# Gate slots of the first activations: 512-column products, four banks, sums on VectorE, and gating on GpSimd

## The chip, the cores and the metric

One core of a Trainium2 chip runs the whole program. The metric is device time in microseconds of one execution; three runs of the kernel before gave a median of 3012.91 us. In the profile, PE is TensorE, PEld its weight loads, DVE is VectorE, ACT is ScalarE, POOL is GpSimd and SP is SyncE.

## The reference, cut to what matters

Two transformer blocks run over 256 tokens of width 2048, all in float32. The second block ends in a mixture of 16384 small experts (PEER). Each token picks 16 experts for each of 8 heads and gates them with a softmax:

```python
act = jax.nn.gelu(jnp.einsum('thkd,td->thk', ub, xb), approximate=False) * gb
vb = jnp.take(v, ib, axis=0)
return jnp.einsum('thk,thkd->td', act.astype(vb.dtype), vb)
```

Here `ub` and `vb` are the rows of `u` and `v` of the chosen experts, `xb` the normed tokens and `gb` the gates.

## The kernel before, in words

The kernel gathers nothing. It computes the activation of every expert for every token (`u` times tokens), multiplies it by a gate that is zero for experts not chosen, and multiplies by all of `v`. The 16384 experts are 128 blocks of 128; a block is one slot. There are two halves of 64 slots each, in the order `peer_u0` (activations of the first half), `peer_v0`, `peer_u1`, `peer_v1`.

**A slot.** SyncE streams a 128x2048 tile of weights into `raw`, with two buffers. Full precision comes from splitting each operand in a high and a low part. ScalarE makes the high part `whi` (L1105), VectorE subtracts to get the low part `wlo` (L1786), and TensorE multiplies whi x high tokens, whi x low tokens and wlo x high tokens, over 16 steps of 128 features. ScalarE may write `whi` of slot n+2 once TensorE has done slot n (`slot_used`), and TensorE starts a slot when its low part is there (`raw_free`).

**Two forms of a slot.** `t_slot` issues three products of 256 columns a step (L523) and puts two slots in one PSUM bank, so that two banks serve in turn. `t2_slot` has the high and the low tokens side by side in `hT2`. It issues one product of 512 columns for whi with both (L536) and one of 256 for wlo (L540), and fills a bank of its own; the two 256-column halves must still be added. `peer_u1` and the query phase `wq` use `t2_slot`, and all of `peer_u0` uses `t_slot`.

**The gates.** In slots 0 to 27 of `peer_u0` (`EARLY` = 28) VectorE selects the experts. In slots 28 to 63, the gate slots, TensorE also makes the gate matrix, beside the activations: 64 groups of four tokens. A group is four products of one-hot rows (L1031) into one of banks 4 to 7. `GATE_COUNT` gives 1 group to slots 28, 29, 35, 42, 49 and 56, 2 to the others and none to slot 63. The products of a group are spread over the steps of the slot by `token_gates`. A group's one-hot rows are written by VectorE in `hot_rows` (L2534 and four of L2539), two groups ahead.

For each group, `weigh` on VectorE (L2547) multiplies the gates of the blocks whose activations are already known into `G`. Then `keep_gates` on ScalarE copies the other gates of this half to `G` (L1612) and those of the second half to a staging buffer (L1614), and sends that to HBM.

**Activations of a pair of slots.** In each even slot VectorE scales the pair before it by the tokens' norm, from PSUM (`scale_acts`, L2447), which also frees the bank. ScalarE computes the gelu of that pair (`gelu_parts`): into `G` for the groups not made yet (L1625), and into `gelu_u` for those already made (L1626). `gate_made` on VectorE then multiplies these with the gates in `G` (L2562), 8 columns for each group made.

**Order of the work.** Each engine works through its program in order. VectorE's iteration for gate slot n is this loop:

```python
for slot in range(EARLY, HALF):
    sum_acts(0, slot - 1)
    if slot in SCALED_AT:
        scale_acts(0, SCALED_AT[slot])
    ...
        split("peer_u0", *divmod(slot + 1, RING))
    ...
    for m in groups_of(slot):
        weigh(m, known_acts(slot))
        ...
            hot_rows(m + 2)
    if slot in SCALED_AT and slot + 2 < HALF:
        gate_made(SCALED_AT[slot], groups_of(slot).stop)
```

`sum_acts` does nothing in `peer_u0` before. ScalarE's iteration is `split` of slot n+1, `keep_gates` of each group of slot n, and in even slots `gelu_parts`. At the start of `peer_v0` ScalarE and VectorE make the first activations' high and low parts (L1651, L2607), and TensorE multiplies them with `v` (L1053), which takes all eight banks. `add_experts`, `gate_pair` and all of the second half stay as they are.

GpSimd has some work in the first block (L1731 to L1742) and four products at the end of the program (L1749).

Of the kernel before, what the change touches and what calls it, by code (L numbers as in the profile page):

```python
# [28 lines left out]
ALU = mybir.AluOpType  # L29
# [52 lines left out]
SUMMED = ("peer_u1",)  # L82
SCALED_AT = {n: n // 2 - 1 for n in range(2, HALF, 2)}
# [78 lines left out]
def fills_per_bank(name, n):  # L162
# [3 lines left out]
    if name in ("in_u", "merge", "nsa_out", "in2_m", "in2_n", "peer_u0", "peer_u1"):  # L166
        return (n, n, 0, 0)
# [16 lines left out]
def build_two_blocks(nc, x, stream, cmpw, params, stage1, mixw_in, fnw1, fnw, gates_dram, out):  # L184
# [6 lines left out]
    with ExitStack() as ctx:  # L191
# [294 lines left out]
        def _(pe):  # L486
# [43 lines left out]
            def t2_slot(name, i, s, ready=None, lo_last=False, middle=None, between=None):  # L530

                t = s % 2
                pe.wait_ge(bank_free[s], i + B0[name][s])
# [502 lines left out]
            for slot in range(EARLY, HALF):  # L1036
                groups = groups_of(slot)
                t_slot("peer_u0", *divmod(slot, RING), (lambda k: token_gates(groups, k)) if groups else None)

            def expert_values(half, i, first, last_group, slots=RING):  # L1040
                name = f"peer_v{half}"
                for s in range(slots):
# [3 lines left out]
                    for b in ((1, 0) if first and s == 0 else (0, 1)):  # L1046
                        if first and s == 0 and b == 0:
                            for e in range(4 if f"peer_u{half}" in SUMMED else 2):
                                pe.wait_ge(bank_free[e], B0[name][e])
# [44 lines left out]
        def _(act):  # L1094
# [478 lines left out]
            def scaled_in(half, p):  # L1573

                i, b = divmod(p, 2)
                if f"peer_u{half}" in SUMMED:
                    act.wait_ge(acts_scaled, HALF // 2 * (half if len(SUMMED) == 2 else 0) + p + 1)
# [140 lines left out]
        def _(pool):  # L1718
# [9 lines left out]
            for c in range(2 * NG):  # L1728
# [14 lines left out]
                pool.wait_ge(pooled, c + 1)  # L1743

# [8 lines left out]
        def _(dve):  # L1753
# [672 lines left out]
            def sum_acts(half, n):  # L2426

                if f"peer_u{half}" in SUMMED:
# [7 lines left out]
                    dve.wait_ge(bank_free[s], B0[f"peer_u{half}"][s] + i + 1)  # L2436

            def scale_acts(half, p):

                i, b = divmod(p, 2)  # L2440
                if f"peer_u{half}" in SUMMED:
# [114 lines left out]
            def gate_made(p, made):  # L2556

                j, b = 2 * p, p % 2
                dve.wait_ge(gelu_done, p + 2)
                dve.wait_ge(g_kept, 4 + made)  # L2560
                gb = G[:, 0:made, j:j + 2, :]
                V.tensor_tensor(gb, gb, gelu_u[:, b, :].rearrange("p (j g t) -> p g j t", j=2, t=4)[:, 0:made],  # L2562
                                ALU.mult).then_inc(gated[b], 1)

            for slot in range(EARLY, HALF):
# [11 lines left out]
                if slot in SCALED_AT and slot + 2 < HALF:  # L2577
                    gate_made(SCALED_AT[slot], groups_of(slot).stop)
# [32 lines left out]
            for half in range(2):  # L2611
# [21 lines left out]
                if half == 0:  # L2633
                    gate_made(HALF // 2 - 2, T // 4)
# [5 lines left out]
                else:  # L2640
                    gate_made(HALF // 2 - 1, T // 4)
# [144 lines left out]
```

## Time and profile before

| | |
|---|---|
| runs, us | 3012.56, 3012.91, 3015.38 |
| the profiled execution, us | 3015.2 |
| its span, us | 3013.3 |
| PE busy | 2959.3 us, 98% |
| PEld busy | 2623.3 us, 87% |
| DVE busy | 1838.7 us, 61% |
| ACT busy | 1262.4 us, 42% |
| POOL busy | 44.9 us, 1% |
| granted TensorE clock, mean | 0.996 of 2.4 GHz |

The time of an execution is a little longer than the span from its first to its last instruction. In a timeline a row has the start in us from the span's start, the duration in us, the engine, the line and operation, output and input, their shapes, and in brackets how long the engine had been idle before and what released it. A count `xN` at the end says that the row merges N instructions. A wait "until issue" had no releaser that the profile shows. Matmuls overlap, so the pitch of whole slots tells more than the duration of one product.

### The profile page before, as it was taken

To read this page: it belongs to the slowest core of one execution; us is meant where nothing else is said; L and a number is where in the kernel's file an instruction comes from. 1 tells how busy PE (TensorE), PEld (TensorE's weight loads), DVE (VectorE), ACT (ScalarE), POOL (GpSimd) and SP (SyncE) were. 2 spreads that over 40 slices of the span, in tenths; PEclk is the share of its full clock that TensorE was granted. 3 is DMA by queue.
4 is the path that set the end of the run, shared out by engine and by line. 5 is a ranking of instruction groups with operands and counts; after the bars stand their busy time and mean duration, and the time that the engine had idled before them with its cause. 6 is when DMAs were issued, how large, how long until landed. Compare 5 with 4: busy or idle time off the path is not lost.

```text
span 3013.3 us, 44793 instructions
## 1 busy us (share of the span) xinstructions
PE 2959.3 (98%) x17931; PEld 2623.3 (87%) x17931; DVE 1838.7 (61%) x2562; ACT 1262.4 (42%) x1518; POOL 44.9 (1%) x63
## 2 busy tenths in 40 slices
PE   7999999999999999999999999999999999999998
PEld 6887899999998888778899999988888888888886
DVE  5555555554555656675899888744445666654444
ACT  4334444443334434444444444444443333344444
POOL 0000013000000000000000000000000000000000
PEclk9999999999999999999999999999999999999999
DMA  5555443334445454335454455555556655555554
GB/s 210 195 202 220 170 158 117 126 141 167 176 171 186 179 195 154 127 139 182 169 181 181 175 172 174 181 195 195 193 190 237 243 187 189 181 195 194 190 190 178
DMA packets 90221, 542.96 MB, mean 180 GB/s; under 512 B 9328, under 2 KB 25840, under 8 KB 26352
## 3 DMA queue, kind: packets, MB, share of 16 engines
q1 hardware_dynamic: 70992, 513.94, 47.4%
q10 hardware_dynamic: 19104, 27.27, 2.6%
q8 instruction: 88, 1.44, 0.2%
q14 instruction: 37, 0.30, 0.0%
HBM read 530.69 MB, written 10.49 MB: 180 GB/s over the span
## 4 chain that ended last, share of the span: by engine, by line
PE 91%; DVE 5%; ACT 2%; issue 1%; DMA 0%; ACTq 0%; SPq 0%; DVEq 0%
PE bank L1053 23%; PE bank L523 22%; PE bank L536 17%; PE bank L540 9%; PE bank L622 8%; PE bank L597 3%; DVE wlo L1786 2%; ACT whi L1105 2%; PE bank L795 2%; PE bank L1031 1%; PE bank L662 1%; PE bank L752 1%; DVE R L2539 0%; PE bank L737 0%; DVE hT L1776 0%
## 5 line engine op out<-in xcount | busy, mean ns | idle before, releaser
L1786 DVE TENSOR_TENSOR wlo<-raw,whi 128x2048 fp32r<-128x2048 f32 (+1 forms) x484 | 1103.7, 2281 | 969.1 <-ACT whi L1105 968.1
L1105 ACT ACTIVATE whi<-raw 128x2048 fp32r<-128x2048 f32 (+1 forms) x484 | 921.2, 1903 | 1320.6 <-PE bank L536 474.3
L523 PE MATMUL bank<-hT,whi 128*128 128x256 f32 x4352 | 823.0, 289 | 0.8 <-DVE wlo L1786 0.8
L536 PE MATMUL bank<-hT,whi 128*128 128x512 f32 x2304 | 804.2, 398 | 3.7 <-DVE wlo L1786 2.9
L523 PEld LDWEIGHTS bank<-hT,whi 128*128 128x128 f32 x4352 | 674.9, 191 | 3.7 <-DVE wlo L1786 1.4
L540 PE MATMUL bank<-hT,wlo 128*128 128x256 f32 x2304 | 622.3, 281 | 1.5 <-DVE wlo L1786 1.2
L523 PE MATMUL bank<-hT,wlo 128*128 128x256 f32 x2176 | 615.3, 283 | 0.0
L536 PEld LDWEIGHTS bank<-hT,whi 128*128 128x128 f32 x2304 | 424.4, 188 | 99.8 <-issue 6.5
L540 PEld LDWEIGHTS bank<-hT,wlo 128*128 128x128 f32 x2304 | 434.0, 189 | 14.4 <-DVE wlo L1786 1.7
L523 PEld LDWEIGHTS bank<-hT,wlo 128*128 128x128 f32 x2176 | 415.4, 191 | 0.0
L1053 PE MATMUL bank<-whi,ghi 128*128 128x512 f32 x1016 | 271.5, 389 | 0.0
L1053 PE MATMUL bank<-wlo,ghi 128*128 128x512 f32 x1016 | 271.5, 389 | 0.0
L1053 PE MATMUL bank<-whi,glo 128*128 128x512 f32 x1016 | 271.5, 389 | 0.0
L622 PE MATMUL bank<-whi,hT 128*128 128x512 f32 x768 | 241.9, 393 | 7.1 <-DVE wlo L1786 3.2
L1053 PEld LDWEIGHTS bank<-whi,glo 128*128 128x128 f32 x1016 | 190.7, 188 | 39.6
L1053 PEld LDWEIGHTS bank<-wlo,ghi 128*128 128x128 f32 x1016 | 190.7, 188 | 39.6
L1053 PEld LDWEIGHTS bank<-whi,ghi 128*128 128x128 f32 x1016 | 190.6, 188 | 39.6
L622 PEld LDWEIGHTS bank<-whi,hT 128*128 128x128 f32 x768 | 145.0, 189 | 40.4 <-issue 9.1
L622 PE MATMUL bank<-wlo,hT 128*128 128x512 f32 x384 | 150.1, 391 | 0.0
L1031 PE MATMUL bank<-R 128*128 128x128 f32 x512 | 99.4, 276 | 1.8 <-DVE R L2539 1.3
L597 PE MATMUL bank<-whi,hT 128*128 128x512 f32 x256 | 85.2, 404 | 0.3 <-ACT R L1422 0.3
L622 PEld LDWEIGHTS bank<-wlo,hT 128*128 128x128 f32 x384 | 72.5, 189 | 14.6
(340 smaller groups left out, 2074.1 us busy)
## 6 DMA issues: line engine op xcount, KB each, us to landing
raw<-stream SPq DMA_DIRECT2D x484, 1024.0 KB, 4.8
R<-cmpw ACTq DMA_DIRECT2D x8, 1024.0 KB, 5.0
gates_dram<-R ACTq DMA_DIRECT2D x64, 128.0 KB, 5.0
R<-gates_dram ACTq DMA_DIRECT2D x16, 512.0 KB, 5.5
xres<-x SPq DMA_DIRECT2D x2, 1024.0 KB, 5.9
R<-mixw ACTq DMA_DIRECT2D x1, 1024.0 KB, 6.8
R<-fnw ACTq DMA_DIRECT2D x1, 1024.0 KB, 6.0
raw<-fnw SPq DMA_DIRECT2D x1, 1024.0 KB, 4.9
```

The costliest lines, as they stand in the source:

```text
L523: last = mm(bank[b][:, t * T:(t + 1) * T], w[t][:, ks], x_[:, k, :], start=(at == 0 and n == 0), stop=(at == KC - 1 and n == 2))
L536: return mm(bank[s][:], whi[t][:, k * P:(k + 1) * P], hT2[:, k, :, :].rearrange("p a t -> p (a t)"), start=(k == 0), stop=(k == KC - 1))
L540: mm(bank[s][:, 0:T], wlo[t][:, k * P:(k + 1) * P], hTh[:, k, :], start=False, stop=False)
L597: last = mm(bank[b][:], x_[:, k, ts_], w[t][:, kk * 512:(kk + 1) * 512], start=(k == 0 and n == 0), stop=(k == KC - 1 and n == 2))
L622: last = mm(bank[2 * h + b][:], x_[:, k, ts_], w[t][:, kk * 512:(kk + 1) * 512], start=(k == 0 and n == 0), stop=(k == KC - 1 and n == 2))
L662: last = mm(bank[6 + v][0:NC4, 0:CH], kb[v][:, l, :], cw[n % 2][:, ll * CH:(ll + 1) * CH], start=(l == 0), stop=(l == CB - 1))
L752: last = mm(o, vN1[:, br, k, kv * DH:(kv + 1) * DH], PT[:, a, j * P:(j + 1) * P], start=False, stop=(j == 2 * nb - 1))
L795: last = mm(bank[s][:, e * T:(e + 1) * T], w[t][:, ks], y[:, k, :], start=(k == 0 and m == 0), stop=(k == 7 and m == 2))
L1031: last = mm(bank[4 + m % 4][:, c * P:(c + 1) * P], second_hot[:, at, :], first_hot[:, at, :], start=True, stop=True)
L1053: last = mm(bank[4 * b + c][:], x_[:, t, ts_], w[t][:, c * 512:(c + 1) * 512], start=(first and s == 0 and n == 0), stop=(last_group and s ...
L1105: A(whi[t][:, 0:w], raw[t][:, 0:w], ACT.Copy).then_inc(hi_ready[t], 1)
L1786: V.tensor_tensor(wlo[t][:, 0:w], raw[t][:, 0:w], whi[t][:, 0:w].bitcast(F32), ALU.subtract).then_inc(raw_free[t], 1)
```

## The change

The gate slots 28 to 63 of `peer_u0` use `t2_slot` instead of `t_slot`. Each fills one of the banks 0 to 3, and VectorE adds the two halves of each (`sum_acts`, a reduction from PSUM to `act_in`); the pair is then scaled in place from SBUF. Slots 0 to 27 keep the old form. The products with the gates (`gate_made`) leave VectorE and are issued on GpSimd, with the same operands, for pairs 13 to 31. The counts of bank fills follow.

```diff
+def summed(half, slot):
+
+    return half == 1 or slot >= EARLY
...
+    if name == "peer_u0":
+        return (n, n, n - EARLY // RING, n - EARLY // RING)
...
-            def t2_slot(name, i, s, ready=None, lo_last=False, middle=None, between=None):
+            def t2_slot(name, i, s, ready=None, lo_last=False, middle=None, between=None, skipped=0):
 
                 t = s % 2
-                pe.wait_ge(bank_free[s], i + B0[name][s])
+                pe.wait_ge(bank_free[s], i + (B0[name][s] - skipped))
...
             for slot in range(EARLY, HALF):
                 groups = groups_of(slot)
-                t_slot("peer_u0", *divmod(slot, RING), (lambda k: token_gates(groups, k)) if groups else None)
+                t2_slot("peer_u0", *divmod(slot, RING), between=(lambda k: token_gates(groups, k)) if groups else None,
+                        skipped=0 if slot % RING < 2 else EARLY // RING)
...
-                            for e in range(4 if f"peer_u{half}" in SUMMED else 2):
+                            for e in range(4):
                                 pe.wait_ge(bank_free[e], B0[name][e])
...
-                if f"peer_u{half}" in SUMMED:
-                    act.wait_ge(acts_scaled, HALF // 2 * (half if len(SUMMED) == 2 else 0) + p + 1)
+                if summed(half, 2 * p):
+                    act.wait_ge(acts_scaled, (HALF // 2 if half else 0) - EARLY // 2 + p + 1)
...
+            for p in range(FIRST_GATED, HALF // 2):
+                j, b, made = 2 * p, p % 2, groups_of(2 * p + 2).stop if 2 * p + 2 < HALF else T // 4
+                pool.wait_ge(gelu_done, p + 2)
+                pool.wait_ge(g_kept, 4 + made)
+                gb = G[:, 0:made, j:j + 2, :]
+                nc.gpsimd.tensor_tensor(gb, gb, gelu_u[:, b, :].rearrange("p (j g t) -> p g j t", j=2, t=4)[:, 0:made],
+                                        ALU.mult).then_inc(gated[b], 1)
...
             def sum_acts(half, n):
 
-                if f"peer_u{half}" in SUMMED:
+                if summed(half, n):
...
-                    dve.wait_ge(bank_free[s], B0[f"peer_u{half}"][s] + i + 1)
+                    dve.wait_ge(bank_free[s], B0[f"peer_u{half}"][s] + i + 1 - (0 if half or s < 2 else EARLY // RING))
...
             def scale_acts(half, p):
...
-                if f"peer_u{half}" in SUMMED:
+                if summed(half, 2 * p):
...
-            def gate_made(p, made):
-
-                j, b = 2 * p, p % 2
-                dve.wait_ge(gelu_done, p + 2)
-                dve.wait_ge(g_kept, 4 + made)
-                gb = G[:, 0:made, j:j + 2, :]
-                V.tensor_tensor(gb, gb, gelu_u[:, b, :].rearrange("p (j g t) -> p g j t", j=2, t=4)[:, 0:made],
-                                ALU.mult).then_inc(gated[b], 1)
...
-                if slot in SCALED_AT and slot + 2 < HALF:
-                    gate_made(SCALED_AT[slot], groups_of(slot).stop)
...
-                if half == 0:
-                    gate_made(HALF // 2 - 2, T // 4)
                 sum_acts(half, HALF - 1)
                 scale_acts(half, HALF // 2 - 1)
                 split(name, 0, 1)
                 if half:
                     gate_pair(HALF // 2 - 1)
-                else:
-                    gate_made(HALF // 2 - 1, T // 4)
```

In `peer_u1`, `sum_acts` and `scale_acts` are those of the second half before, L2433 and L2443 in the profile.

## Rows read from the trace of the kernel before

**Rows 1.** Waits, 1675 to 1942 us: total us, times, longest us.

```profile
DVE wlo L1786 <- ACT whi L1105: 37.4, 35, 1.6
...
DVE R L2547 <- PE bank L1031: 5.1, 7, 1.9
PEld bank L1031 <- issue: 3.9, 12, 0.5
```

**Rows 2.** Timeline of ScalarE before slot 28: start us, us, what.

```profile
1657.74 1.92 ACT L1105 ACTIVATE whi<-raw 128x2048 fp32r<-128x2048 f32 x1 [1.90 <-PE bank L523]
1663.51 1.92 ACT L1105 ACTIVATE whi<-raw 128x2048 fp32r<-128x2048 f32 x1 [3.84 <-PE bank L523]
```

**Rows 3.** Timeline of ScalarE in the query phase, first two slots, 512-column products.

```profile
1422.20 1.92 ACT L1105 ACTIVATE whi<-raw 128x2048 fp32r<-128x2048 f32 x1 [0.61 <-PE bank L536]
1427.75 1.92 ACT L1105 ACTIVATE whi<-raw 128x2048 fp32r<-128x2048 f32 x1 [3.63 <-PE bank L536]
```

**Rows 4.** Timeline of ScalarE in the second half's activations, 512-column products.

```profile
2309.48 1.92 ACT L1105 ACTIVATE whi<-raw 128x2048 fp32r<-128x2048 f32 x1 [3.21 <-PE bank L536]
...
2315.12 1.92 ACT L1105 ACTIVATE whi<-raw 128x2048 fp32r<-128x2048 f32 x1 [3.73 <-PE bank L536]
```

**Rows 5.** Timeline of VectorE: its iterations 32, 33 and 62 begin.

```profile
1706.08 0.69 DVE L2447 TENSOR_TENSOR R<-bank,token_scale 128x512 f32<-128x512 f32 x1
1707.53 2.29 DVE L1786 TENSOR_TENSOR wlo<-raw,whi 128x2048 fp32r<-128x2048 f32 x1 [0.77 <-ACT whi L1105]
...
1713.64 0.23 DVE L2562 TENSOR_TENSOR R<-R 128x64 f32<-128x64 f32 x1 [0.18 <-ACT R L1626]
1715.44 2.29 DVE L1786 TENSOR_TENSOR wlo<-raw,whi 128x2048 fp32r<-128x2048 f32 x1 [1.58 <-ACT whi L1105]
...
1931.38 0.68 DVE L2447 TENSOR_TENSOR R<-bank,token_scale 128x512 f32<-128x512 f32 x1
1932.73 2.29 DVE L1786 TENSOR_TENSOR wlo<-raw,whi 128x2048 fp32r<-128x2048 f32 x1 [0.67 <-ACT whi L1105]
```

**Rows 6.** Timeline of ScalarE at the end of gate slot 32.

```profile
1713.37 0.24 ACT L1626 ACTIVATE R<-R 128x64 f32<-128x64 f32 x1
1713.51 1.90 ACT L1105 ACTIVATE whi<-raw 128x2048 fp32r<-128x2048 f32 x1
```

**Rows 7.** Timeline of VectorE: weighings that waited for TensorE, three of seven.

```profile
1688.85 0.27 DVE L2547 TENSOR_TENSOR R<-bank,R 128x112 f32<-128x112 f32 x1 [0.41 <-PE bank L1031]
...
1733.36 0.30 DVE L2547 TENSOR_TENSOR R<-bank,R 128x136 f32<-128x136 f32 x1 [0.39 <-PE bank L1031]
...
1890.39 0.38 DVE L2547 TENSOR_TENSOR R<-bank,R 128x216 f32<-128x216 f32 x1 [0.31 <-PE bank L1031]
```

**Rows 8.** Timeline of TensorE's weight loads: three of its twelve gaps.

```profile
1719.68 0.30 PEld L1031 LDWEIGHTS bank<-R 128*128 128x128 f32 x2 [0.23 <-issue]
...
1869.24 0.30 PEld L1031 LDWEIGHTS bank<-R 128*128 128x128 f32 x2 [0.42 <-issue]
...
1929.63 0.30 PEld L1031 LDWEIGHTS bank<-R 128*128 128x128 f32 x2 [0.51 <-issue]
```

**Rows 9.** Timeline of VectorE in the second half: a sum and a scaling.

```profile
2303.77 0.69 DVE L2433 TENSOR_REDUCE R<-bank 128x256 f32<-128x512 f32 x1 [2.16 <-PE bank L536]
2304.50 0.69 DVE L2443 TENSOR_TENSOR R<-R,token_scale 128x512 f32<-128x512 f32 x1
```

**Rows 10.** GpSimd's groups by line and shape: x count, busy us, mean ns.

```profile
L1749 POOL TENSOR_TENSOR R<-xres,raw 128x512 f32<-128x512 f32 x4 | 5.0, 1288 | 2516.5 <-DVE xres L2654 2516.5
```

**Rows 11.** Timelines of GpSimd and of VectorE, an overlap in the first block.

```profile
455.88 2.34 POOL L1731 COPY R<-R 128x256 f32<-128x256 f32 x1
...
455.12 2.85 DVE L1786 TENSOR_TENSOR wlo<-raw,whi 128x2048 fp32r<-128x2048 f32 x1 [3.00 <-ACT whi L1105]
```

**Rows 12.** Timelines of VectorE and of TensorE at the start of peer_v0.

```profile
1940.68 0.75 DVE L2607 TENSOR_TENSOR glo<-R,ghi 128x256 fp32r<-128x256 f32 x2
...
1942.24 1.09 PE L1053 MATMUL bank<-whi,ghi 128*128 128x512 f32 x4
```

More of the change, by code:

```diff
@@ L165, in fills_per_bank @@
         return (n,) * 4
-    if name in ("in_u", "merge", "nsa_out", "in2_m", "in2_n", "peer_u0", "peer_u1"):
+    if name == "peer_u0":
+        return (n, n, n - EARLY // RING, n - EARLY // RING)
+    if name in ("in_u", "merge", "nsa_out", "in2_m", "in2_n"):
         return (n, n, 0, 0)
```

## The prediction

> **What bounds the kernel.** I read the page's busy shares first: TensorE is busy for 98% of the span at a granted clock of 2.4 GHz in every slice, so only TensorE's own time, or a wait of TensorE, can move the end. Then I read the stretch that the change touches, the 36 gate slots (28 to 63), from about 1675 to 1942 us. The waits there [rows 1] hold the argument. TensorE's weight loads had twelve gaps, 3.9 us together, so the stretch isn't bound by TensorE alone. ScalarE and VectorE hand work round in a ring, and this ring sets the pace of most slots: VectorE's low part of a slot waits for ScalarE's high part 35 times, 37.4 us; VectorE in turn waited for TensorE only 7 times, 5.1 us.
>
> The ring, for slot n: VectorE weighs the slot's last group (L2547); ScalarE keeps the rest of that group, in even slots computes the pair's gelu, and then makes the high part of slot n+2's weights (L1105); VectorE makes their low part (L1786), weighs slot n+1's first group and makes the one-hot rows for slot n+2's first group (L2534, L2539); TensorE's first gate product of slot n+2 needs these rows. Every gap of TensorE is at that product, in an even slot: [rows 8] show those of slots 34, 54 and 62, growing from 0.23 to 0.51 us.
>
> The reader should see two things in VectorE's timeline [rows 5]. In each iteration of its loop VectorE stands idle before L1786, 0.77 and 0.67 us in even iterations and 1.58 us in odd ones, always released by ScalarE. And the gating product that the change takes away (L2562) lies in the odd hole, behind ScalarE's gelu and before that wait.
>
> **TensorE's part.** A slot goes from 48 products of 256 columns to 16 of 512 and 16 of 256. The same columns pass, so the price is read from the pitch of whole slots. A slot of the old form is 1663.51 − 1657.74 = 5.77 us [rows 2], one of the new form 2315.12 − 2309.48 = 5.64 us in the second half [rows 4] and 5.55 us in the query phase [rows 3]. The second half streams the same kind of weights through the same loop of waits, so I take its row, rounded down with the 5.76 of most old slots to 0.11 us a slot, 0.007 us for each of 16 steps; the query phase's 0.21 is the other bound. The 256 gate products are untouched. If TensorE alone set the pace, this would be 36 × 0.11 = 4.0 us (7.6 by the other bound).
>
> It doesn't. What TensorE saves before one of the twelve gaps makes that gap longer: the one-hot rows come when the ring brings them. A saving counts only where the ring itself waited for TensorE. That is so in seven places, of which [rows 7] show three:
> - Slots 28 and 29, before the first gap: 2 × 0.11 = 0.22 us, under the wait of 0.41 in slot 29.
> - The four slots with one group in the middle (35, 42, 49, 56), where VectorE waited 0.39, 0.46, 0.30 and 0.31 us; [rows 7] have the first and the last of these four. From the last gap before each, TensorE has run 30 or 46 steps (slot 34 to 35, [rows 8], is 14 + 16; slot 54 to 56 is 14 + 32), so it arrives 0.21, 0.32, 0.21 and 0.32 us earlier. None may exceed its wait: 0.21 + 0.32 + 0.21 + 0.31 = 1.05 us.
> - After the last gap, in slot 62, TensorE runs freely to the end of slot 63: 30 steps, 0.21 us.
>
> Together −1.5 us. By 0.21 us a slot it would be 0.41 + (0.39 + 0.46 + 0.30 + 0.31) + 0.39 = 2.3 us.
>
> **VectorE's additions.** Each slot gets a sum of the two halves, 0.69 us, and the next operation starts 0.73 us after it because its completion is awaited (2304.50 − 2303.77, [rows 9]). The scaling stays at 0.69 us, now from SBUF: the same [rows 9]. That is 36 × 0.73 = 26 us of added work, and it costs what doesn't fit in the holes. Even iterations: sum and scaling need 0.73 + 0.69 = 1.42 us from where the scaling began; L1786 started 1707.53 − 1706.08 = 1.45 us after that point at the start and 1932.73 − 1931.38 = 1.35 us at the end [rows 5]. So it fits early and is up to 0.07 us too long late; neighbours on VectorE overlap a little, so I take 0.2 us over all 17, between 0 and 17 × 0.07 = 1.2. Odd iterations: the sum waits for the gelu of the pair before (it overwrites that input), which ends at 1713.37 + 0.24 = 1713.61 [rows 6]; 0.73 us later is 1714.34, and L1786 starts at 1715.44 [rows 5] because ScalarE's high part ends then. 1.1 us remain: cost 0. The cover is ScalarE's 1.90 us high part; if it were gone, each odd iteration would pay the 0.73.
>
> Taking the 19 gating products from VectorE (0.23 us for 64 columns, [rows 5]) gives nothing: VectorE went from each into a wait for ScalarE (1.58 us), and ScalarE waited for none of them.
>
> **Banks.** Slots now use four banks in turn; a bank is needed again four slots later and is freed one slot later. 0. At the start of peer_v0 TensorE begins with banks 4 to 7 and needs banks 0 to 3 only after twelve products; four of them take 1.09 us [rows 12], so about 3 us later. The last sum and nothing else is late by 0.73 us: 0.
>
> **GpSimd's products.** GpSimd stood idle here. No row shows a product of this shape (runs of 4 and 8 elements); the nearest is a plain one of 512 columns at 1.29 us [rows 10], 2.5 ns a column. The products have 8 columns for each group made, 8 to 480 in the loop and 512 twice. Each starts when its gelu ends (1713.61) and, if it keeps VectorE out, must be over when L1786 starts (1715.44): 1.83 us, of which I allow 0.1 to start. At 1.29 or less, that is 0. Does it keep VectorE out? [Rows 11] show that the two engines exclude each other for some pairs of operations: a GpSimd copy of 256 columns took 2.34 us and ended with VectorE's low part (455.12 + 2.85 = 457.97), which itself was stretched from 2.29 to 2.85 us. The Trainium skill says so in "SBUF — State Buffer", Who interferes with whom: a VectorE operation with two SBUF inputs and a GpSimd one that reads SBUF exclude each other for a whole instruction, while a reduction on this chip never contends. By that rule the new sum passes beside GpSimd, and the total below stands as it is; the trace agrees for L1786, and has no row for a sum. If the sum were held up too, it would end at 1713.7 + 1.3 + 0.7 = 1715.7 us, 0.3 late, where the product has all 1.29 us, so in the last two or three odd iterations: 0.6 us. I take 0 of it, since a sum reads PSUM alone, and keep 0.6 for the range.
>
> One place is tight. The product of pair 30 starts while VectorE is about to make peer_v0's first low activations (L2607, two in 0.75 us from 1940.68, [rows 12]). TensorE wants the first at 1942.24, now 0.2 us earlier, about 0.9 us after it was ready. A GpSimd product of 1.29 us that slips in ahead would cost 0.4 us, one that doesn't 0. I take 0.1. Later, the waits for gated pairs lie more than a slot after GpSimd's last product: 0.
>
> **Sum.** −1.5 + 0.2 + 0.1 = −1.2 us. The profiled execution has a span of 3013.3 us and a time of 3015.2, which is 2.3 above the median of the runs, 3012.91. The difference is carried to the median: **3011.7 us**, with 3010.6 (−2.3) to 3013.6 (−1.5 + 1.2 + 0.4 + 0.6) for this case from the ends of its terms.
>
> **Rivals.**
> - *The ring gives way.* If VectorE's side without gating made the one-hot rows early enough, the gaps would go and TensorE's saving would be whole: −4.0 − 3.9 = −7.9, 3005.0 us. It would need 0.2 to 0.5 us less in each round. Against it: nothing on ScalarE's side gets shorter, and VectorE waits for ScalarE in 35 of 36 iterations [rows 1].
> - *The sum lies on the ring in even iterations.* If the hole of 0.67 to 0.77 us were not to be had (the sum starting late, or the scaling waiting), 17 × 0.73 = 12.4 us: 3012.9 − 1.2 + 12.4 = 3024 us. It decides once a round grows by 0.42 us. For it: the hole is full to 0.1 us. Against it: the sum's products end well before VectorE comes to it, so it has nothing to wait for.
> - *GpSimd's products outlast the hole.* At twice the plain row (5 ns a column) the five products from 360 to 480 columns average 2.1 us, 0.4 over the 1.7 free, and pair 30's costs 1.7 at the entry: +3.7, 3015.4 us. At three times, nine products exceed it by 1.0 each and the entry pays 3.0: +12, 3024 us. It decides at about 2.4 times. For it: [rows 11], and that no such shape was ever timed. Against: runs of 4 contiguous elements.
>
> **How the numbers follow.** Forecast 0.73; the ring gives way 0.07; the sum on the ring 0.07; GpSimd at up to 2.4 times 0.08, beyond it 0.05. A measurement of this kernel tells a difference from none at about 0.2%, 6 us. Faster than 3006.9: 0.07. Slower than 3018.9: 0.12. Within: 0.81. The range runs from 3007.5, towards the ring's giving way, to 3016.5, past GpSimd's twofold price, and leaves out under 2 in 10.
>
> **What would show it.** L536 and L540 in place of L523 in this stretch, and old-form slots' 5.76 against 5.65 us where no gap is. TensorE's weight loads with twelve or more gaps, each in an even slot, each longer by about 0.1 to 0.2 us, so some 6 us in total instead of 3.9. VectorE's idle before L1786 near 0 in even iterations and about 0.9 in odd ones, still released by ScalarE. GpSimd's products at 1.3 us or less for 480 columns, and L1786 at 2.29 us. I am wrong if L1786 is stretched or released by GpSimd, if the rounds of two slots (7.91 us from 1707.53 to 1715.44 for the first half of one, [rows 5]) change by more than 0.1 us, or if the gaps vanish.

## The result and the profile after

Before: median 3014.39 us of 20 runs (3011.43 to 3016.94). After: 3018.89 us of 20 runs (3015.17 to 3023.32). The ratio is 1.0016, with a 95% interval of 1.0009 to 1.0023: the change makes the kernel slower, by 2.7 to 6.9 us. The forecast was a gain of 1.2 us, and the range ended at 3016.5. The three runs that the forecast started from had a median 1.5 us below that of the twenty, so the difference is the number to explain.

The profiled execution took 3017.41 us with a span of 3015.6 us, against 3015.2 and 3013.3 before, at the same mean granted clock of 0.996. The two traces are laid side by side at six marks: VectorE's first scaling of the gate slots, its last weighing in slot 62, TensorE's first product of `peer_v0`, of `peer_u1` and of `peer_v1`, and VectorE's last operation of the program.

| stretch | before, us | after, us | difference |
|---|---|---|---|
| gate slots (first scaling to last weighing) | 259.26 | 259.46 | +0.20 |
| entry to `peer_v0` (last weighing to first product) | 5.55 | 7.75 | +2.20 |
| `peer_v0` | 349.14 | 349.22 | +0.08 |
| `peer_u1` | 362.28 | 362.29 | +0.01 |
| `peer_v1` | 351.48 | 351.45 | −0.03 |

The loss in these two traces is in two places, 2.4 us together: most of it at the entry, and a small one where a gain was forecast. The waits of after, from 1675 to 1942 us, answer to [rows 1]. Columns: engine, what waits, what ended the wait; total us, times, longest.

```profile
DVE wlo L1804 <- ACT whi L1115: 18.9, 17, 1.1
...
PEld bank L1040 <- issue: 7.1, 12, 0.8
DVE R L2451 <- ACT R L1636: 7.0, 18, 3.4
DVE R L2565 <- PE bank L1040: 4.2, 7, 1.8
```

TensorE's gaps are still twelve but hold 7.1 us instead of 3.9. VectorE waits for ScalarE before its low part 17 times instead of 35, so the even iterations have no idle left there, and only the odd ones (1.1 us each) do. VectorE's wait for TensorE fell only from 5.1 to 4.2. And there is a new line: the sum (L2451) waits for ScalarE's gelu (L1636), once for as long as 3.4 us. The page's row for TensorE's first product of an expert block (`expert_values`, L1063), with its one idle time at the end:

```profile
L1063 PE MATMUL bank<-whi,ghi 128*128 128x512 f32 x1016 | 271.6, 389 | 2.1 <-DVE glo L2614 2.1
```

**The entry.** VectorE's timeline in after, from the end of iteration 62, against the same in [rows 12]. Columns: start us, us, engine and line, shapes, and in brackets the idle time before and what ended it.

```profile
1936.73 0.41 DVE L2565 TENSOR_TENSOR R<-bank,R 128x240 f32<-128x240 f32 x1 [1.26 <-PE bank L1040]
1940.58 0.69 DVE L2451 TENSOR_REDUCE R<-bank 128x256 f32<-128x512 f32 x1 [3.44 <-ACT R L1636]
1941.30 2.69 DVE L1804 TENSOR_TENSOR wlo<-raw,whi 128x2048 fp32r<-128x2048 f32 x1
1943.92 0.75 DVE L2614 TENSOR_TENSOR glo<-R,ghi 128x256 fp32r<-128x256 f32 x2
```

ScalarE, GpSimd and TensorE at the same place, one view each:

```profile
1936.57 1.92 ACT L1115 ACTIVATE whi<-raw 128x2048 fp32r<-128x2048 f32 x1 [0.60 <-PE bank L545]
...
1939.86 0.62 ACT L1636 ACTIVATE R<-R 128x512 f32<-128x512 f32 x1
```

```profile
1940.55 1.29 POOL L1760 TENSOR_TENSOR R<-R 128x512 f32<-128x512 f32 x1 [15.73 <-ACT R L1636]
1946.74 2.61 POOL L1760 TENSOR_TENSOR R<-R 128x512 f32<-128x512 f32 x1 [4.90 <-ACT R L1636]
```

```profile
1944.48 1.17 PE L1063 MATMUL bank<-whi,ghi 128*128 128x512 f32 x4 [2.13 <-DVE glo L2614]
```

Before, the same place has these rows of VectorE and of ScalarE:

```profile
1938.47 2.29 DVE L1786 TENSOR_TENSOR wlo<-raw,whi 128x2048 fp32r<-128x2048 f32 x1 [1.38 <-ACT whi L1105]
```

```profile
1939.82 0.62 ACT L1626 ACTIVATE R<-R 128x512 f32<-128x512 f32 x1
```

In after, ScalarE had the high part of `peer_v0`'s first weights ready at 1938.5. Before, VectorE made the low part there, at 1938.47. Now iteration 63 begins with the sum of slot 62. It writes over the input of pair 30's gelu, and that gelu is not made in iteration 62, as those of other pairs are in their even iteration: `slot + 2 < HALF` fails for slot 62, and ScalarE makes it at the entry, after `keep_gates` and the high activations. So the sum starts at 1940.58. The low part starts 2.83 us later than before and takes 2.69 instead of 2.29 us beside GpSimd's product. The low activations start at 1943.92 instead of 1940.68, and TensorE stands still for 2.13 us.

**The gate slots.** VectorE in iterations 32, 33 and 62 of after answers to [rows 5]:

```profile
1705.90 0.69 DVE L2451 TENSOR_REDUCE R<-bank 128x256 f32<-128x512 f32 x1
1706.62 0.69 DVE L2461 TENSOR_TENSOR R<-R,token_scale 128x512 f32<-128x512 f32 x1
1707.36 2.29 DVE L1804 TENSOR_TENSOR wlo<-raw,whi 128x2048 fp32r<-128x2048 f32 x1
...
1713.54 0.69 DVE L2451 TENSOR_REDUCE R<-bank 128x256 f32<-128x512 f32 x1 [0.24 <-ACT R L1636]
1715.34 2.29 DVE L1804 TENSOR_TENSOR wlo<-raw,whi 128x2048 fp32r<-128x2048 f32 x1 [1.11 <-ACT whi L1115]
...
1931.51 0.69 DVE L2451 TENSOR_REDUCE R<-bank 128x256 f32<-128x512 f32 x1
1932.23 0.69 DVE L2461 TENSOR_TENSOR R<-R,token_scale 128x512 f32<-128x512 f32 x1
1932.86 2.29 DVE L1804 TENSOR_TENSOR wlo<-raw,whi 128x2048 fp32r<-128x2048 f32 x1
```

The even iterations are as forecast: sum and scaling fill the hole, and the low part starts 1932.86 − 1931.51 = 1.35 us after the start of this work, the same as 1.35 in [rows 5]. In the odd ones VectorE has 1.11 us left and is released by ScalarE, also as forecast. Yet look at when it is released. ScalarE's timeline of after has the high part of this slot at

```profile
1713.34 1.90 ACT L1115 ACTIVATE whi<-raw 128x2048 fp32r<-128x2048 f32 x1
```

so the low part starts 2.00 us after the high part did. Before it was 1715.44 − 1713.51 = 1.93 us [rows 5, 6]. It is 2.00 or 2.01 in all 17 odd iterations of after, and 1.93 in all 17 of before. TensorE's weight loads, the gaps of slots 34, 54 and 62, answer to [rows 8]:

```profile
1719.58 0.30 PEld L1040 LDWEIGHTS bank<-R 128*128 128x128 f32 x2 [0.58 <-issue]
...
1869.37 0.30 PEld L1040 LDWEIGHTS bank<-R 128*128 128x128 f32 x2 [0.77 <-issue]
...
1929.76 0.30 PEld L1040 LDWEIGHTS bank<-R 128*128 128x128 f32 x2 [0.82 <-issue]
```

### The profile page after: what moved, and what is told of

Read it like the earlier page. It is cut to its first block, busy times and chain, and to the rows that moved or that the text cites. A ratio compares the mean times of both kernels' runs of the same rounds, so it can differ in the third digit from the quotient of the medians.

```text
span 3015.6 us, 43714 instructions
## 1 busy us (share of the span) xinstructions
PE 2956.9 (98%) x17355; PEld 2593.9 (86%) x17355; DVE 1855.4 (62%) x2579; ACT 1262.4 (42%) x1518; POOL 61.0 (2%) x82
## 4 chain that ended last, share of the span: by engine, by line
PE 89%; DVE 6%; ACT 3%; issue 1%; DMA 0%; ACTq 0%; DVEq 0%; SPq 0%
PE bank L1063 23%; PE bank L545 19%; PE bank L532 18%; PE bank L549 10%; PE bank L631 8%; PE bank L606 3%; DVE wlo L1804 2%; ACT whi L1115 2%; PE bank L804 2%; PE bank L671 1%; DVE R L2557 1%; PE bank L1040 1%; PE bank L761 1%; DVE R L2552 0%; PE bank L746 0%
## 5 line engine op out<-in xcount | busy, mean ns | idle before, releaser
L545 PE MATMUL bank<-hT,whi 128*128 128x512 f32 x2880 | 1021.0, 398 | 3.9 <-DVE wlo L1804 3.0
L545 PEld LDWEIGHTS bank<-hT,whi 128*128 128x128 f32 x2880 | 533.7, 188 | 113.7 <-issue 7.4
L532 PE MATMUL bank<-hT,whi 128*128 128x256 f32 x3200 | 585.5, 285 | 0.8 <-DVE wlo L1804 0.8
L532 PEld LDWEIGHTS bank<-hT,whi 128*128 128x128 f32 x3200 | 498.2, 192 | 3.6 <-DVE wlo L1804 1.4
L1063 PE MATMUL bank<-whi,ghi 128*128 128x512 f32 x1016 | 271.6, 389 | 2.1 <-DVE glo L2614 2.1
L1063 PE MATMUL bank<-wlo,ghi 128*128 128x512 f32 x1016 | 271.5, 389 | 0.0
L1063 PE MATMUL bank<-whi,glo 128*128 128x512 f32 x1016 | 271.5, 389 | 0.0
L631 PE MATMUL bank<-whi,hT 128*128 128x512 f32 x768 | 242.1, 393 | 7.3 <-DVE wlo L1804 3.2
L1063 PEld LDWEIGHTS bank<-whi,ghi 128*128 128x128 f32 x1016 | 190.6, 188 | 41.9 <-issue 2.4
L1063 PEld LDWEIGHTS bank<-wlo,ghi 128*128 128x128 f32 x1016 | 190.7, 188 | 39.7
L1063 PEld LDWEIGHTS bank<-whi,glo 128*128 128x128 f32 x1016 | 190.7, 188 | 39.6
L2451 DVE TENSOR_REDUCE R<-bank 128x256 f32<-128x512 f32 x100 | 69.0, 690 | 69.4 <-PE bank L545 62.3
L1040 PEld LDWEIGHTS bank<-R 128*128 128x128 f32 x512 | 95.3, 189 | 17.1 <-issue 7.1
```

The lines of the kernel that those rows point to most:

```text
L532: last = mm(bank[b][:, t * T:(t + 1) * T], w[t][:, ks], x_[:, k, :], start=(at == 0 and n == 0), stop=(at == KC - 1 and n == 2))
L545: return mm(bank[s][:], whi[t][:, k * P:(k + 1) * P], hT2[:, k, :, :].rearrange("p a t -> p (a t)"), start=(k == 0), stop=(k == KC - 1))
L631: last = mm(bank[2 * h + b][:], x_[:, k, ts_], w[t][:, kk * 512:(kk + 1) * 512], start=(k == 0 and n == 0), stop=(k == KC - 1 and n == 2))
L1040: last = mm(bank[4 + m % 4][:, c * P:(c + 1) * P], second_hot[:, at, :], first_hot[:, at, :], start=True, stop=True)
L1063: last = mm(bank[4 * b + c][:], x_[:, t, ts_], w[t][:, c * 512:(c + 1) * 512], start=(first and s == 0 and n == 0), stop=(last_group and s ...
L2451: last = V.tensor_reduce(act_in[half][:, n % 2 * T:n % 2 * T + T], bank[s][:].rearrange("p (a t) -> p t a", a=2), AX.X, ALU.add)
```

## The experiments

Parts of the trace are given as gate slots and entry, by the marks of the table above. The gate slots begin up to 4 us earlier or later in one execution than in another, so only differences within one trace are compared, not its absolute times. Ratios are to the kernel before; each carries its 95% interval. Three groups of kernels shared the before runs of their chip: medians 3014.91 (the first four), 3015.05 (the next four) and 3014.87 us (the last three).

### e1_entry: the last sum leaves iteration 63

```diff
             for slot in range(EARLY, HALF):
-                sum_acts(0, slot - 1)
+                if slot + 1 < HALF:
+                    sum_acts(0, slot - 1)
...
                     low_acts(half, 0, s)
+                if half == 0:
+                    sum_acts(half, HALF - 2)
                 sum_acts(half, HALF - 1)
```

> The changed kernel with one order changed on VectorE: the sum of slot 62 leaves iteration 63 and comes after the low activations of peer_v0, just before the sum of slot 63. Theory (entry): the change loses its time at the start of peer_v0, where the sum of slot 62 waits for the gelu of pair 30, which ScalarE only makes after the high activations; VectorE's low part of peer_v0's first weights stands behind that wait, and TensorE stood 2.2 us for it in the profile (its last old product ended near 1942.2, L1063 began at 1944.48). Then that gap falls to 0 to 0.4 us (GpSimd's product may still slip in) and the span comes back to about 3013.3 to 3013.7. Rival 1 (the sums on the ring in even iterations) and rival 2 (GpSimd holding VectorE's port) both leave the time at 4 to 5 us over the kernel before, with L1804 in peer_v0 still late or the gaps of the gate slots carrying the loss.

Measured: 3014.16 us, ratio 0.9998 (0.9989 to 1.0007); gate slots 259.37, entry 5.69 us. The loss at the entry is gone but for 0.14 us, and neither rival's 4 to 5 us is there. GpSimd's product now gets in ahead of the low activations; by itself it costs 0.11 us there (e3_pool_only). VectorE's timeline, then GpSimd's:

```profile
1937.23 2.29 DVE L1804 TENSOR_TENSOR wlo<-raw,whi 128x2048 fp32r<-128x2048 f32 x1 [1.38 <-ACT whi L1115]
1939.44 1.88 DVE L2615 TENSOR_TENSOR glo<-R,ghi 128x256 fp32r<-128x256 f32 x2
```

```profile
1939.27 1.43 POOL L1760 TENSOR_TENSOR R<-R 128x512 f32<-128x512 f32 x1 [15.75 <-ACT R L1636]
```

### e2_gate_dve: the gating product back on VectorE

The loop over pairs on GpSimd is taken out, and VectorE gets it where the kernel before has it:

```diff
                         hot_rows(m + 2)
+                if slot in SCALED_AT and slot + 2 < HALF:
+                    gate_made(SCALED_AT[slot], groups_of(slot).stop)
...
                     low_acts(half, 0, s)
+                if half == 0:
+                    gate_made(HALF // 2 - 2, T // 4)
...
+                else:
+                    gate_made(HALF // 2 - 1, T // 4)
```

> The changed kernel with the gating products back on VectorE, all else kept, the entry order too. Entry theory: the wait of the sum of slot 62 stays, so most of the loss stays; only the 0.4 us by which GpSimd stretched the low part at the entry (2.69 against 2.29 us) goes, while VectorE's own products of 0.23 to 0.68 us lie in the odd holes, which the sums leave 1.1 us wide: 1.5 to 2 us over the kernel before in the span. GpSimd rival: the time falls to that of the kernel before or below. Ring rival: stays at 4 to 5 us over.

Measured: 3017.01 us, ratio 1.0009 (0.9999 to 1.0018); gate slots 259.43, entry 7.34 us. Of the 2.20 us at the entry, 1.79 stay without GpSimd; its lock on the low part is the other 0.4. In the gate slots, where VectorE makes the product, nothing changes (0.03 us), as the forecast had it.

### e3_pool_only: the kernel before with gating on GpSimd

```diff
+            for p in range(FIRST_GATED, HALF // 2):
+                j, b, made = 2 * p, p % 2, groups_of(2 * p + 2).stop if 2 * p + 2 < HALF else T // 4
+                pool.wait_ge(gelu_done, p + 2)
+                pool.wait_ge(g_kept, 4 + made)
...
-                if slot in SCALED_AT and slot + 2 < HALF:
-                    gate_made(SCALED_AT[slot], groups_of(slot).stop)
```

> The kernel before with the gating products alone on GpSimd (old form of slots, no sums in this half). Entry theory: nothing but up to 0.4 us at the entry of peer_v0, so no measurable difference (within 1 us of before). GpSimd rival: 2 to 5 us slower than before, with L1786 stretched or released by GpSimd in the gate slots.

Measured: 3015.06 us, ratio 1.0005 (0.9996 to 1.0014); gate slots 259.25, entry 5.66 us. So the move to GpSimd alone costs 0.11 us at the entry and nothing before it.

### e4_wait_only: the kernel before with the wait alone

```diff
                 else:
+                    dve.wait_ge(gelu_done, HALF // 2)
                     split("peer_v0", 0, 0)
```

> The kernel before with one wait added: in iteration 63 VectorE waits for the gelu of pair 30 before it makes the low part of peer_v0's first weights. Nothing else differs. Entry theory: that low part starts near 1940.5 instead of 1938.47, the first low activations are ready near 1943.1 and TensorE starts peer_v0 near 1943.2 instead of 1942.24: 1.0 us longer; the sum (0.7) and the stretch by GpSimd (0.4) make up the rest of the 2.2 us in the changed kernel. The rivals say nothing happens here: the loss is in the gate slots.

Measured: 3015.73 us, ratio 1.0003 (0.9993 to 1.0012); gate slots 259.24, entry 6.55 us, so +1.00. VectorE's timeline has the wait in the place where after has it. This execution reached the gate slots 3.96 us later than before did (1681.39 against 1677.43), so 1944.41 answers to the 1940.5 that was expected:

```profile
1944.41 2.29 DVE L1786 TENSOR_TENSOR wlo<-raw,whi 128x2048 fp32r<-128x2048 f32 x1 [3.37 <-ACT R L1626]
```

The wait alone is 1.00, the 0.7 us of the sum behind it make 1.79 (e2_gate_dve), and GpSimd's lock 2.20. Behind the wait nothing hides a step any more, and each adds about what it takes on VectorE. The timed ratios are too coarse to tell these steps apart.

### f1_order_old: the kernel before, ScalarE's gelu after the next high part

If the ring between ScalarE and VectorE sets the pace, taking something out of it must close the gaps, with the products as they were.

```diff
+                if slot - 1 in SCALED_AT and slot - 1 >= EARLY and slot + 1 < HALF:
+                    gelu_parts(SCALED_AT[slot - 1], groups_of(slot - 1).stop)
                 for m in groups_of(slot):
...
                     keep_gates(m, known_acts(slot))
-                if slot in SCALED_AT and slot + 2 < HALF:
-                    gelu_parts(SCALED_AT[slot], groups_of(slot).stop)
```

VectorE's `gate_made` moves with it, to the end of the odd iteration, and its wait to the start of that iteration.

> The kernel before (old form of slots, gating on VectorE) with the ring of the gate slots shortened: ScalarE makes the high part of slot n+2 first and then the gelu of the pair, one iteration later than before, and VectorE does the gating product at the end of the odd iteration. If the ring of ScalarE and VectorE makes TensorE's twelve gaps (3.9 us in the weight loads, some 5 us with what follows them), taking the gelu (0.8 us) out of the odd rounds closes all of them: the gate stretch falls from 259.3 by 4 to 5 us, to about 254.5, and the time by as much. If the gaps have another cause, nothing changes.

Measured: 3010.75 us, ratio 0.9985 (0.9976 to 0.9994); gate slots 254.40 us, 4.9 less, and no gap of TensorE. Its waits, of the same stretch as [rows 1]:

```profile
DVE wlo L1786 <- ACT whi L1105: 32.0, 34, 1.4
...
DVE R L2547 <- PE bank L1031: 8.8, 7, 1.9
```

VectorE still waits for ScalarE in 34 iterations. These waits don't say that ScalarE sets the end: both engines are now ahead of TensorE. What tells the two apart is the gap of TensorE, and that VectorE's wait for TensorE grew from 5.1 to 8.8 us.

### f2_order_new and f3_order_pool: this order under the new products

Both start from e1_entry and take f1's order. VectorE now does both sums of a pair ahead of the scaling, because the gelu that frees the first half's place comes later. f2_order_new has the gating on VectorE, f3_order_pool on GpSimd.

```diff
-                if slot + 1 < HALF:
+                if slot % 2 == 0:
                     sum_acts(0, slot - 1)
...
+                late = slot - 1 in SCALED_AT and slot - 1 >= EARLY and slot + 1 < HALF
...
+                if late:
+                    gate_made(SCALED_AT[slot - 1], groups_of(slot - 1).stop)
+                if late:
+                    sum_acts(0, slot - 1)
```

> The same reordering on the new form: 512-column products, four banks, sums on VectorE (the odd one at the end of its iteration), gating on VectorE, and the sum of slot 62 out of the way of peer_v0. By the ring theory TensorE's own saving of 0.11 us a slot now counts as well, as far as VectorE keeps up (its rounds reach about 14.9 us a pair late, TensorE's are 14.7): the stretch falls by 7 to 8 us to about 252, and the time to 3007 where before is at 3014.4. If TensorE's saving was never real with gate products between, the result equals that of the reordered old form.

> The reordered new form with the gating products on GpSimd. They now start while VectorE works (low part and one-hot rows, both with two SBUF inputs). If the two engines exclude each other for whole instructions, VectorE's L2534-type rows or the weighings after them start up to 1.3 us late in odd iterations, more as the product grows, and most of the gain is lost late in the stretch: 2 to 6 us slower than the same order with gating on VectorE. If they don't exclude each other, it is equal or up to 1 us faster, since VectorE has 0.2 to 0.65 us less to do.

Measured: 3018.46 us, ratio 1.0007 (0.9998 to 1.0016), and 3019.18 us, ratio 1.0013 (1.0004 to 1.0022); gate slots 263.40 and 262.71 us. Both forecasts were missed: the order that took 4.9 us out of the gate slots under the old products adds 4.1 and 3.5 us to them here, and the kernel with GpSimd is not the slower one in this stretch. VectorE's timeline of f2_order_new shows what differs:

```profile
1856.92 0.49 DVE L2572 TENSOR_TENSOR R<-R 128x328 f32<-128x328 f32 x1
1857.33 1.41 DVE L2443 TENSOR_REDUCE R<-bank 128x256 f32<-128x512 f32 x2
1858.78 0.69 DVE L2453 TENSOR_TENSOR R<-R,token_scale 128x512 f32<-128x512 f32 x1
1859.39 2.29 DVE L1796 TENSOR_TENSOR wlo<-raw,whi 128x2048 fp32r<-128x2048 f32 x1
...
1866.78 2.29 DVE L1796 TENSOR_TENSOR wlo<-raw,whi 128x2048 fp32r<-128x2048 f32 x1 [1.30 <-ACT whi L1115]
```

All the added work stands in one place, 2.47 us between the hot rows and the low part of the even iteration, and the hole of the odd one stands empty with 1.30 us. TensorE has 10.4 us of gaps. That the one place is the cause is only a reading here; g1_balanced puts it to the test.

In f3_order_pool GpSimd's product of the same pair waits for the low part and then holds up a hot-row operation. GpSimd's row, then VectorE's:

```profile
1854.76 2.40 POOL L1760 TENSOR_TENSOR R<-R 128x328 f32<-128x328 f32 x1 [11.59 <-ACT R L1636]
```

```profile
1856.59 1.12 DVE L2552 TENSOR_TENSOR R<-par,R 128x512 f32<-128x512 f32 x1
```

It takes 0.49 us off VectorE and stretches the hot-row operation from 0.68 to 1.12 us, so the two nearly cancel in this pair. Over the whole stretch it is 0.69 us less than f2_order_new, and at the entry 0.54 more (6.21 against 5.67).

### g1_balanced: one sum in each iteration

From f2_order_new. A second buffer for the activations' input (`other_acts`) lets the sum of an even slot go ahead before the gelu of the pair before it is made. Then each iteration starts with one sum, and the gating product stands in the odd one, a pair later.

```diff
+        other_acts = region(sc_at + 5120, 2 * T)
+        def act_pair(half, p):
+            return other_acts if half == 0 and p >= EARLY // 2 and p % 2 == 0 else act_in[half]
...
-                        dve.wait_ge(gelu_done, HALF // 2 * half + n // 2 + 1)
+                        dve.wait_ge(gelu_done, HALF // 2 * half + n // 2 + (1 if half else 0))
...
-                if slot % 2 == 0:
+                if slot % 2 and slot - 3 >= EARLY:
+                    gate_made(SCALED_AT[slot - 3], groups_of(slot - 3).stop)
+                if slot + 1 < HALF:
                     sum_acts(0, slot - 1)
...
-                if late:
-                    gate_made(SCALED_AT[slot - 1], groups_of(slot - 1).stop)
-                if late:
-                    sum_acts(0, slot - 1)
```

> The reordered new form again, with VectorE's additions spread over both holes. The input of the gelu gets a second buffer, so that the sum of an even slot needn't wait for the gelu of the pair before; each iteration begins with one sum, even ones also scale, and odd ones also do the gating product of the pair of three slots before. In f2_order_new the odd hole stood 1.3 us empty while 2.6 us of gating, two sums and scaling filled the other. If that imbalance was what made it slow, VectorE now has about 1.4 us in each hole, the stretch falls to 251 to 254 us (TensorE alone would need 250.3: 254.4 of the reordered old form less 36 times 0.11) and the time is 1 to 4 us below the reordered old form. If 512-column products beside gate products save nothing on TensorE, the stretch stays at 254.4 or above.

Measured: 3007.67 us, ratio 0.9974 (0.9965 to 0.9984), 7.8 us (4.8 to 10.6) under the kernel before. Gate slots 251.71 us. VectorE's timeline of an even and an odd iteration:

```profile
1850.89 0.68 DVE L2448 TENSOR_REDUCE R<-bank 128x256 f32<-128x512 f32 x1
1851.60 0.69 DVE L2458 TENSOR_TENSOR R<-R,token_scale 128x512 f32<-128x512 f32 x1
1852.27 2.29 DVE L1801 TENSOR_TENSOR wlo<-raw,whi 128x2048 fp32r<-128x2048 f32 x1
...
1858.29 0.48 DVE L2577 TENSOR_TENSOR R<-R 128x328 f32<-128x328 f32 x1
1858.70 0.68 DVE L2448 TENSOR_REDUCE R<-bank 128x256 f32<-128x512 f32 x1
1859.74 2.29 DVE L1801 TENSOR_TENSOR wlo<-raw,whi 128x2048 fp32r<-128x2048 f32 x1 [0.37 <-ACT whi L1120]
```

Its waits have two gaps of TensorE left:

```profile
DVE wlo L1801 <- ACT whi L1120: 9.9, 19, 0.9
DVE R L2562 <- PE bank L1045: 7.3, 7, 1.8
...
PEld bank L1045 <- issue: 0.4, 2, 0.2
```

Against f1_order_old, which is as near to TensorE's own pace but has the old products, the gate slots take 254.40 − 251.71 = 2.7 us less, 3.1 without the two gaps. That is TensorE's saving when it is let through, as near as these two kernels tell; the forecast's 0.11 us a slot would make 35 × 0.11 = 3.9 us.

### h1_own_wait: the sum's completion awaited later

From e1_entry. In odd iterations VectorE no longer waits for its own sum before the low part, but before the scaling of the next iteration, which reads it.

```diff
                     last.then_inc(bank_free[s], 1)
-                    dve.wait_ge(bank_free[s], B0[f"peer_u{half}"][s] + i + 1 - (0 if half or s < 2 else EARLY // RING))
+                    if half or n % 2:
+                        dve.wait_ge(bank_free[s], B0[f"peer_u{half}"][s] + i + 1 - (0 if half or s < 2 else EARLY // RING))
...
+                    if half == 0:
+                        s0 = 2 * p % RING
+                        dve.wait_ge(bank_free[s0], B0["peer_u0"][s0] + i + 1 - (0 if s0 < 2 else EARLY // RING))
```

> The kernel of e1_entry, in which VectorE in odd iterations no longer waits for the completion of its own sum at once, but one iteration later, before the scaling that reads it. In the changed kernel L1804 starts 2.00 us after the start of ScalarE's high part in odd iterations, against 1.93 us before, 0.07 us in each of 17 rounds, 1.2 us: what ate TensorE's saving. If the awaited completion ahead of the next wait is the cause, the lag returns to 1.93 and the stretch falls from 259.4 to about 258.2; if a reduction itself delays the next operation, both stay.

Measured: 3014.59 us, ratio 1.0002 (0.9993 to 1.0011); gate slots 258.35 us against 259.37 in e1_entry, so 1.0 less, and gaps of 6.2 us. VectorE's and then ScalarE's row of slot 33's low and high part:

```profile
1715.57 2.29 DVE L1804 TENSOR_TENSOR wlo<-raw,whi 128x2048 fp32r<-128x2048 f32 x1 [1.04 <-ACT whi L1115]
```

```profile
1713.64 1.90 ACT L1115 ACTIVATE whi<-raw 128x2048 fp32r<-128x2048 f32 x1
```

1.93 us again, in all 17 odd iterations. The wait moved and nothing else did. 17 × 0.07 = 1.2 us should go with it; the stretch is 1.0 us shorter.

### f4_changed_again and g0_order_again: the same kernels once more

Both are unchanged copies, of the changed kernel and of f1_order_old.

> The changed kernel once more, beside the others. Its profile showed 2.4 us more than before in the gate slots and the entry of peer_v0 (0.20 and 2.20), the measured ratio 1.0016 gave 4.8 us with an interval from 2.7. If the profile tells all, the ratio here comes out near 1.0008; if something outside these stretches costs too, near 1.0016 again, and the profile shows a third stretch that is longer.

> The reordered old form once more, to stand beside g1_balanced on the same chip: 4 to 5 us below the kernel before, as the first time (stretch 254.4 us).

Measured: 3017.80 us, ratio 1.0010 (1.0001 to 1.0019), with gate slots 259.44 and entry 7.76 us; and 3009.19 us, ratio 0.9984 (0.9975 to 0.9993), with gate slots 254.41 us. The parts of the trace repeat within 0.02 us; the whole times do not. That is why the causes above are read from the parts.

## Why the prediction was wrong

**The step that failed** is in "Banks": "The last sum and nothing else is late by 0.73 us: 0." I had the wait of the sum for the gelu of the pair before, and costed it in the odd iterations by [rows 6], where that gelu ends just before VectorE comes to it. I took iteration 63 for one of these. In it the gelu is the one that ScalarE makes at the entry, at 1939.82 before, behind four other operations. So the sum waits 3.44 us, and behind it on VectorE's queue stands the low part of `peer_v0`'s first weights, and behind that the low activations that TensorE needs. This was to be had from the trace of before: gelu done about 1940.5, plus 0.73 for the sum, against 1938.47 for the low part there, 2.8 us late. TensorE stood ready about 0.9 us after the low activations before, so some 1.9 of it would have come through. It measured 1.79, and 2.20 with GpSimd. The forecast had looked at GpSimd alone in this place, for 0.1 us. Between its −1.2 us and the 2.4 of the parts lie 3.6: 2.1 are this place, 1.2 and 0.5 the next two terms, less the 0.2 of the even iterations.

**Odd iterations: cost 0.** Right in what ends the wait and in the 1.1 us left, wrong by 0.07 us each, 1.2 us in all. An engine with an idle hole is not free of every cost inside it. h1_own_wait shows the cause: with the completion of the sum awaited in the hole, the low part that waits next for ScalarE starts 0.07 us later. It costs this although it is long over.

**TensorE's saving in seven places, −1.5 us.** The mechanism was right: VectorE's wait in slot 29 fell from 0.41 to 0.25 us and that of slot 35 from 0.39 to 0.16, and the gaps grew in place of the rest: ten of the twelve by 0.29 to 0.39 us each, where 0.1 to 0.2 was forecast, and those of slots 44 and 58 not at all. Of this sum the part up to slot 62 is 0.22 + 1.05 + 0.10 = 1.4 us; VectorE's waits for TensorE fell by 0.9 us, and h1_own_wait, where the odd iterations' 0.07 is away, stands 259.26 − 258.35 = 0.9 us below the kernel before. So it was taken too high by about 0.5. The nearest cause for the size is the pitch: 2.7 to 3.1 us for the whole stretch in g1_balanced is 0.08 to 0.09 us a slot, not 0.11. In the five slots (29, 35, 42, 49, 56) the waits of h1_own_wait are about 1.0 us shorter, where 1.27 was forecast; against it stand 0.4 us of waits for TensorE in slots 30, 36 and 50 that the forecast did not have.

**Even iterations, +0.2.** 0: the low part starts 1.35 us after the work before it, as before. **Gating taken off VectorE, 0.** Right (e2_gate_dve against after, 0.03 us). **Gaps of 6 us.** 7.1; without the 0.07 they are 6.2.

**GpSimd's products.** In size and place as forecast: 0.32 us for 64 columns and 1.24 for 480, so runs of 4 and 8 elements cost no more than the plain 1.29 us for 512, and every one in the loop is over before the low part starts. That the sum isn't held by them holds too. GpSimd's and VectorE's rows in after:

```profile
1923.58 1.24 POOL L1760 TENSOR_TENSOR R<-R 128x480 f32<-128x480 f32 x1 [14.41 <-ACT R L1636]
```

```profile
1923.61 0.69 DVE L2451 TENSOR_REDUCE R<-bank 128x256 f32<-128x512 f32 x1 [0.15 <-ACT R L1636]
```

This also agrees with the rule of the Trainium skill that was cited ("SBUF — State Buffer", Who interferes with whom). Pair 30's product cost 0.11 us at the entry of e3_pool_only, and the forecast's 0.1 is luck there: it was a mean of two cases. The product did slip in ahead, the two low activations took 1.86 instead of 0.75 us, and the forecast had put 0.4 on that case. In after it met the low part itself, and cost 0.4. That stretched low part is one of the forecast's own signs of being wrong; the rounds, at 7.98 instead of 7.91 us, stayed inside the 0.1 that it allowed.

**The rivals.** The ring did not give way, and neither the sum in even iterations nor GpSimd outlasted its hole. f1_order_old and g1_balanced show that the first rival's end was real all the same: a round is tied to the order in which ScalarE makes gelu and high part, not to VectorE's gating. Its 7.9 us and the 7.8 of g1_balanced agree in part by luck: the rival put 3.9 us on the gaps and 4.0 on the products, and in the gate slots they measured 4.9 and 2.7.

**What stays open.** The parts of the trace give 2.4 us, in two executions of the changed kernel. Its 20 runs gave 4.5 (2.7 to 6.9), and the 11 of f4_changed_again 3.0 (0.3 to 5.7). For the rest the granted clock is the nearest explanation. Executions of one kernel with a lower mean clock took longer. Of 31 of the changed kernel the median is 3017.7 us at a mean clock of 0.996 of 2.4 GHz (14 of them) and 3023.0 at 0.994 (5). Of the 92 of the kernel before that stand beside the experiments it is 3015.0 at 0.996 (41) and 3019.2 at 0.994 (6). At 0.996 the two kernels are 2.8 us apart, near the 2.4 of the parts. In the profiled executions this time lies ahead of the gate slots: e4_wait_only, at 0.994, began them 4.0 us later than before, and its granted clock from 700 to 1300 us was 0.98 instead of 0.99. Clocks of 0.995 or 0.994 were 13 of the 20, then 2 of the 11, against 30 of the 92; whether the change itself makes them more frequent isn't shown. Why the wait in the odd iterations costs its 0.07 us stays open too.

## What to carry to other kernels

When an operation with a wait is put at the head of an engine's loop, work out the wait for the last iteration too: the guards of the loop (`slot + 2 < HALF`) move its producer elsewhere, and behind it stands the start of the next stage. A faster product on TensorE gives little while another ring of engines makes gaps in it: 0.9 us in h1_own_wait, 2.7 with the gaps closed. First close the ring by order (f1_order_old, −4.9 us), then spread the work that the faster form adds over all holes: under the same order of ScalarE, the sums and the gating in one hole lost 4.1 us in the gate slots against before, and spread over both they won 7.6.

## What the runs showed of the hardware

- An operation of VectorE that waits for another engine started 2.00 us after ScalarE's operation did, where VectorE awaited the completion of its own last operation in the same hole, and 1.93 us without that wait (after and h1_own_wait, 17 iterations each), though that completion was over a microsecond old.
- GpSimd and VectorE exclude each other where VectorE reads two operands from SBUF, whichever is first: the low part took 2.69 instead of 2.29 us, two low activations 1.88 instead of 0.75 (e1_entry), a hot-row operation 1.12 instead of 0.68 (f3_order_pool), and GpSimd's 512 columns 2.61 instead of 1.29 us behind a low part. The reduction from PSUM kept its 0.69 us.
